# Norms in a two-block transformer kernel: adding squares on VectorE, fewer steps behind the sums, and rows moved behind the heads' step

## The reference, cut to what matters

```python
def rms_norm(x, w):
    y = x * lax.rsqrt(jnp.mean(x * x, axis=-1, keepdims=True) + NORM_EPS)
    return y * w

def modulate(x, g, shift, scale):
    return rmsnorm(x, g) * (1.0 + scale) + shift

def l2norm(t):                       # queries and keys of the delta net, per head
    return t * lax.rsqrt(jnp.sum(t * t, axis=-1, keepdims=True) + EPS)
```

## Time and profile before

| | |
|---|---|
| median of 3 runs | 3462.91 us (3462.8 to 3464.23) |
| profiled execution: its own time | 3464.78 us |
| profiled execution: span | 3463.0 us |
| mean granted clock of PE | 0.967 |
| busy: PE, DVE, ACT, POOL | 3294.6, 2049.1, 1328.1, 528.5 us |

### The profile page before, as it was taken

How to read it: one execution, slowest core, us unless ns; L and a number is a source line. 1 busy time by engine, 2 the same in 40 slices (tenths; PEclk the granted TensorE clock), 3 DMA queues, 4 the chain that set the end, 5 groups by cost and what they waited for, 6 DMA issues and landing times.

```text
span 3463.0 us, 41094 instructions
## 1 busy us (share of the span) xinstructions
PE 3294.6 (95%) x16321; PEld 2722.7 (79%) x16321; DVE 2049.1 (59%) x3543; ACT 1328.1 (38%) x2338; POOL 528.5 (15%) x547
## 2 busy tenths in 40 slices
PE   8999999999999999999899997899898999999998
PEld 5764889998888888888788875778686667778887
DVE  5765987776888888887555435445443345443332
ACT  3131238883444444444322224444443124232221
POOL 0001009971222222221000000000000000000000
PEclk9999999999999999999899998999899999999999
DMA  6426234569999999996355422121121122222222
GB/s 253 138 70 221 74 123 173 191 218 345 335 329 333 338 330 327 338 327 250 105 187 183 144 70 91 58 86 67 64 83 55 41 82 79 90 79 96 96 94 75
DMA packets 190207, 574.42 MB, mean 166 GB/s; under 512 B 16576, under 2 KB 82112, under 8 KB 171712
## 3 DMA queue, kind: packets, MB, share of 16 engines
q1 hardware_dynamic: 152144, 367.96, 30.4%
q0 software_dynamic: 37872, 203.84, 16.0%
HBM read 523.89 MB, written 47.84 MB: 165 GB/s over the span
## 4 chain that ended last, share of the span: by engine, by line
PE 84%; DVE 9%; ACT 3%; POOL 2%; DMA 1%; issue 1%; SPq 0%; DVEq 0%; ACTq 0%; POOLq 0%
PE ps L231 11%; PE ps L232 10%; PE ps L233 10%; PE ps L1602 5%; PE ps L1603 5%; PE ps L1601 5%; PE ps L1362 4%; PE ps L1364 4%; PE ps L1363 4%; PE ps L240 4%; PE ps L581 2%; PE ps L316 2%; PE ps L171 1%; DVE Wl L223 1%; PE ps L584 1%; POOL peerg_OH L1354 1%
## 5 line engine op out<-in xcount | busy, mean ns | idle before, releaser
L223 DVE TENSOR_TENSOR Wl<-W,Wh 128x1024 fp32r<-128x1024 f32 x363 | 438.6, 1209 | 706.5 <-ACT Wh L217 700.3
L217 ACT ACTIVATE Wh<-W 128x1024 fp32r<-128x1024 f32 x363 | 377.6, 1041 | 567.2 <-PE ps L233 532.1
L1362 PE MATMUL ps<-peer_Hh,Wh 128*128 128x384 f32 x1024 | 349.5, 341 | 8.9 <-DVE Wl L223 8.9
L1364 PE MATMUL ps<-peer_Hh,Wl 128*128 128x384 f32 x1024 | 346.3, 338 | 0.0
L1363 PE MATMUL ps<-peer_Hl,Wh 128*128 128x384 f32 x1024 | 346.0, 338 | 0.0
L1570 POOL DMA_INDIRECT peerv_UV<-peer_uv,peer_EX x128 | 209.8, 1639 | 641.1 <-DVE peer_Y L1638 583.5
L1601 PE MATMUL ps<-peerv_VH,peer_HTh 128*128 128x512 f32 x768 | 299.0, 389 | 2.2 <-DVE peer_HTl L1664 2.2
L1603 PE MATMUL ps<-peerv_VH,peer_HTl 128*128 128x512 f32 x768 | 300.5, 391 | 0.0
L1602 PE MATMUL ps<-peerv_VL,peer_HTh 128*128 128x512 f32 x768 | 300.3, 391 | 0.0
L231 PE MATMUL ps<-f_Hh,Wh 128*128 128x512 f32 x672 | 262.3, 390 | 2.2 <-DVE Wl L223 2.2
L233 PE MATMUL ps<-f_Hh,Wl 128*128 128x512 f32 x672 | 261.5, 389 | 0.0
(11 more groups left out here) (497 smaller groups left out, 6499.3 us busy)
## 6 DMA issues: line engine op xcount, KB each, us to landing
W<-peer_u SPq DMA_DIRECT2D x128, 512.0 KB, 8.0
peerv_VR<-peer_v SPq DMA_DIRECT2D x128, 512.0 KB
gates_dram<-peerg_GB SPq DMA_DIRECT2D x12, 2048.0 KB, 7.3
peerv_GR<-gates_dram SPq DMA_DIRECT2D x32, 768.0 KB, 8.6
f_AW<-w_ada POOLq DMA_DIRECT2D x48, 512.0 KB, 4.2
W<-w_gate SPq DMA_DIRECT2D x44, 512.0 KB, 3.2
W<-w_up SPq DMA_DIRECT2D x44, 512.0 KB, 3.2
swa_AW<-w_ada POOLq DMA_DIRECT2D x32, 512.0 KB, 4.5
```

Of the source, the lines that this page charges most:

```text
L217: A.then_inc(e.activation(w_parts(i)[0], w_raw(i), ACT.Copy), ("w_hi", i))
L223: V.then_inc(e.tensor_tensor(lo, w_raw(i), hi.bitcast(F32), SUB), ("w", i))
L1362: e.matmul(o, hi[:, k, :], H2[0][:, k, 0:TD], start=k == 0, stop=False)
L1364: ins = e.matmul(o, lo[:, k, :], H2[0][:, k, 0:TD], start=False, stop=k == 7)
```

## The change

- In six norms DVE adds most squares onto the first one (`add_dve`, a tensor_tensor of 128x512), and PE sums that one tile, called S, beside the rows named in `order`. n2, m2, f2 and ne sum S and row 7 (8 matmuls in place of 32); nf and f1 sum rows 2, 5, 7 and then S (16). n1 keeps all eight rows. All of a norm's matmuls accumulate into four PSUM columns. Row 0 has a slot of its own, the others alternate between two.
- `mean_dve` goes. ACT's root reads the sums in PSUM itself, with 1/D as its scale and epsilon as its bias (a column set once at the start). The diagonal is made in four tensor_scalar of 128x128, and PE broadcasts each quarter as soon as it is there.
- In the loops the blocks of the squares leave their places between the tiles and stand behind the loop.
- In stage delta a row now has two halves on DVE and ACT, and the heads' step stands between them: weight tile, scaling and root first; then the heads; then convolution (DVE), silu, square or drain (ACT). PE's order stays. The root of the rows' norm reads PSUM too, without DVE's addition of epsilon (L2117).

```diff
     class Norm:
...
         def square(self, k):
-            return DG_t[:, 512 * (k % 3):512 * (k % 3) + 512]
+            at = 512 * (k % 2 + 1) if k else 0
+            return DG_t[:, at:at + 512]

         def sq_act(self, e, k):
             self.ready(e, k)
-            if k >= 3:
-                PE.wait_ge(e, (self.tag, "sq", k - 3))
+            if k - 2 in self.adds:
+                V.wait_ge(e, (self.tag, "add", k - 2))
+            elif k > 2:
+                PE.wait_ge(e, (self.tag, "sq", k - 2))
             A.then_inc(e.activation(self.square(k), X[:, k, :], ACT.Square), (self.tag, "sq", k))

+        def add_dve(self, e, k):
+            if k in self.adds:
+                A.wait_ge(e, (self.tag, "sq", k))
+                if k > self.adds[0]:
+                    V.wait_ge(e, (self.tag, "add"))
+                V.then_inc(e.tensor_tensor(self.square(0), self.square(0), self.square(k), ADD), (self.tag, "add", k),
+                           (self.tag, "add"))
+
         def sq_pe(self, e, k):
-            A.wait_ge(e, (self.tag, "sq", k))
+            if k == "S":
+                V.wait_ge(e, (self.tag, "add", self.adds[-1]))
+            else:
+                A.wait_ge(e, (self.tag, "sq", k))
             for tb, sl in enumerate(sl4):
-                ins = e.matmul(self.bank[:, 8 * tb + k:8 * tb + k + 1], self.square(k)[:, sl], ones[:, 0:1],
-                               start=True, stop=True)
+                ins = e.matmul(self.bank[:, tb:tb + 1], self.square(0 if k == "S" else k)[:, sl], ones[:, 0:1],
+                               start=k == self.order[0] and tb == 0, stop=k == self.order[-1], skip_group_check=True)
             PE.then_inc(ins, (self.tag, "sq", k))

-        def mean_dve(self, e):
...
         def root_act(self, e):
-            V.wait_ge(e, (self.tag, "mean"))
-            A.then_inc(e.activation(self.s, self.s, ACT.Sqrt), (self.tag, "root"))
+            V.wait_ge(e, "eps")
+            PE.wait_ge(e, (self.tag, "sq", self.order[-1]))
+            A.then_inc(e.activation(self.s, self.bank[:, 0:4], ACT.Sqrt, bias=eps1, scale=1.0 / D), (self.tag, "root"))

         def root_dve(self, e):
             A.wait_ge(e, (self.tag, "root"))
             V.then_inc(e.reciprocal(self.s, self.s))
             V.wait_ge(e, V.n)
-            V.then_inc(e.tensor_tensor(v4(self.square(8)), bc4(ident), self.s.unsqueeze(2).broadcast_to([128, 4, 128]),
-                                       MUL), (self.tag, "diag"))
+            for tb, sl in enumerate(sl4):
+                V.then_inc(e.tensor_scalar(self.square(8)[:, sl], ident, self.s[:, tb:tb + 1], None, MUL),
+                           (self.tag, "diag", tb))

         def root_pe(self, e):
-            V.wait_ge(e, (self.tag, "diag"))
-            PE.then_inc(e.matmul(self.bank, ones, self.square(8), start=True, stop=True), (self.tag, "rstd"))
+            for tb, sl in enumerate(sl4):
+                V.wait_ge(e, (self.tag, "diag", tb))
+                PE.then_inc(e.matmul(self.bank[:, sl], ones, self.square(8)[:, sl], start=True, stop=True),
+                            (self.tag, "rstd"))
...
     def wout1_pe(e):
...
-            if nb >= 4:
-                n2n.sq_pe(e, nb - 4)
         ada2a.pe(e, 2)
-        for k in range(4, 8):
+        for k in n2n.order:
             n2n.sq_pe(e, k)
     def wout1_dve(e):
...
             for n in range(3 * nb, 3 * nb + 3):
                 ada2a.mac(e, n)
+            n2n.add_dve(e, nb - 1)
             PE.wait_ge(e, ("wout1", nb))
             residual(e, nb, mod1[:, 16:24], ps(4 + nb % 4), ("x1", nb))
...
     def fin_dve(e):
...
             residual(e, k, mod1[:, 40:48], ps(FIN_BANK[k]), ("x2", k))
+            nf.add_dve(e, k - 2)
+        nf.add_dve(e, 6)
         ff1.scales(e)
-        nf.mean_dve(e)
         nf.root_dve(e)
         for k in range(8):
             nf.scale_dve(e, k, X[:, k, :], vec("final_norm_w"), ("x3", k))
+            f1n.add_dve(e, k - 2)
+        f1n.add_dve(e, 6)
...
@@ FeedForward.pe, and wout2_pe alike
-                if nb >= 2:
-                    then.sq_pe(e, nb - 2)
-            then.sq_pe(e, 6)
-            then.sq_pe(e, 7)
+            for k in then.order:
+                then.sq_pe(e, k)
...
@@ FeedForward.dve
                 if n % 3 == 2:
+                    then.add_dve(e, n // 3 - 1)
                     self.x(e, n // 3)
             for nb in range(len(rest) // 3, 8):
+                then.add_dve(e, nb - 1)
                 self.x(e, nb)
@@ wout2_dve
             w_lo(e, (t_wo2 + ff2.all)[n + 2])
+            f2n.add_dve(e, n - 1)
             PE.wait_ge(e, ("wout2", n))
             residual(e, n, mod2[:, 40:48], ps(n % 4), ("x4", n))
...
     def row_steps(rows, make_head):
...
             live = [g for g in live if next(g, "end") != "end"]
+            if rows:
+                next(rows)
     def rows_act(e):
...
-                V.wait_ge(e, ("nr1", m))
-                A.then_inc(e.activation(r, r, ACT.Sqrt), ("nr2", m))
+                if m >= 3:
+                    V.wait_ge(e, ("ndg", m - 3))
+                PE.wait_ge(e, ("nsum", m))
+                A.then_inc(e.activation(r, ps(6 + m % 2)[:, 0:4], ACT.Sqrt, bias=eps1), ("nr2", m))
+            yield
             if n < NROW:
                 kind, h, c = ROWS[n]
     def rows_dve(e):
...
-                PE.wait_ge(e, ("nsum", m))
-                V.then_inc(e.tensor_scalar(r, ps(6 + m % 2)[:, 0:4], 1.0, EPS, MUL, ADD), ("nr1", m))
                 A.wait_ge(e, ("nr2", m))
...
+            yield
             if n < NROW and ROWS[n][0] == "qkv":
                 _, h, c = ROWS[n]
```

More of the change, by code:

```diff
@@ L248, in build @@
     cs1, cs2 = tiny(8), tiny(8)
+    eps1 = tiny(1)
     def mac(e, acc, w, cs, k):
@@ L300, in build, with __init__ @@
     class Norm:
-        def __init__(self, tag, bank, ready):
-            self.tag, self.bank, self.ready, self.s = tag, ps(bank), ready, tiny(4)
+        def __init__(self, tag, bank, ready, order):
+            self.tag, self.bank, self.ready, self.s, self.order = tag, ps(bank), ready, tiny(4), order
+            self.adds = [k for k in range(1, 8) if k not in order]
         def square(self, k):
-            return DG_t[:, 512 * (k % 3):512 * (k % 3) + 512]
+            at = 512 * (k % 2 + 1) if k else 0
+            return DG_t[:, at:at + 512]
@@ L361, in dve @@
         def dve(self, e):
-            self.norm.mean_dve(e)
             self.norm.root_dve(e)
@@ L421, in build @@
     w1 = tiny(8)
-    n1 = Norm("n1", 0, lambda e, k: x_in.wait_ge(e, "x"))
-    n2n = Norm("n2", 0, lambda e, k: V.wait_ge(e, ("x1", k)))
+    n1 = Norm("n1", 0, lambda e, k: x_in.wait_ge(e, "x"), range(8))
+    n2n = Norm("n2", 0, lambda e, k: V.wait_ge(e, ("x1", k)), ("S", 7))
     PA = Phase("ada")
@@ L513, in ada1_dve @@
     def ada1_dve(e):
+        V.then_inc(e.memset(eps1, EPS), "eps")
         con_in.wait_ge(e, "con")
@@ L1713, in fin_pe @@
             PE.then_inc(ins, ("yt", k))
-        for k in range(8):
+        for k in nf.order:
             nf.sq_pe(e, k)
         nf.root_pe(e)
-        for k in range(8):
+        for k in f1n.order:
             f1n.sq_pe(e, k)
@@ L1802, in act, with dve @@
                 then.sq_act(e, k)
-        def dve(self, e, ahead):
+        def dve(self, e, then, ahead):
             tag = self.tag
@@ L2177, in keys_act @@
             yield
+            yield
     def keys_dve(e):
-        yield
-        yield
+        for _ in range(4):
+            yield
         PE.wait_ge(e, ("nbc", 15))
         lat_norm_dve(e, "k", 2, 6)
+        for _ in range(4):
+            yield
+        lat_scale_dve(e, "k", KL, 2, "g_kv_lat_2", 7)
         yield
-        yield
-        lat_scale_dve(e, "k", KL, 2, "g_kv_lat_2", 7)
         yield
@@ L2894, in wout2_pe @@
             pe_three(e, ps(nb % 4), t_wo2[nb], 8, 128, YP, 0, 8, ("wout2", nb))
-            if nb >= 2:
-                f2n.sq_pe(e, nb - 2)
-        f2n.sq_pe(e, 6)
-        f2n.sq_pe(e, 7)
+        for k in f2n.order:
+            f2n.sq_pe(e, k)
     def wout2_act(e):
@@ L2945, in vector @@
         for tag, stage in (("ada1", ada1_dve), ("swa", mix1_dve), ("wout1", wout1_dve),
-                           ("query", query_dve), ("gates", gates_dve), ("dense", dense_dve), ("fin", fin_dve),                            ("ffn1", lambda e: ff1.dve(e, t_ab)), ("mix2", mix2_dve), ("delta", delta_dve), ("state", state_dve),
+                           ("query", query_dve), ("gates", gates_dve), ("dense", dense_dve), ("fin", fin_dve),                            ("ffn1", lambda e: ff1.dve(e, m2n, t_ab)), ("mix2", mix2_dve), ("delta", delta_dve), ("state", state_dve),
                            ("heads", heads_dve),
-                           ("b2", b2_dve), ("wout2", wout2_dve), ("ffn2", lambda e: ff2.dve(e, [])), ("end", end_dve)):
+                           ("b2", b2_dve), ("wout2", wout2_dve), ("ffn2", lambda e: ff2.dve(e, ne, [])), ("end", end_dve)):
             if tag in on:
```

16 lines of the change are left out of this document (5 added, 11 removed).

## The result

| | before | changed |
|---|---|---|
| median of the runs | 3462.86 us (4 runs) | 3410.70 us (4 runs, 3408.83 to 3412.17) |
| profiled execution, span | 3464.78, 3463.0 us | 3408.83, 3406.9 us |
| busy: PE, DVE, ACT | 3294.6, 2049.1, 1328.1 us | 3249.2, 2064.8, 1330.2 us |

The ratio is 0.9855, with a 95% interval from 0.9839 to 0.9871. The prediction was 3415, in a range from 3400 to 3433: 47.8 us of gain were forecast, 52.2 came. The terms of the sum did less well than the sum, as the experiments show.

The account below looks back on a forecast made before the run. PE, busy 95% of the span, was taken to bound the kernel. Norms 32.8 us plus rows 15 gave 47.8 of gain: 3415 us against a median of 3462.9, range 3400 to 3433.

Parts of the forecast that it names:

- Blocks in the stream: m2, f2, ne, n2: square-sum blocks (four matmuls per row) leave the dense stream at 0.9 each, gaining 13.5 plus 2.7 us.
- n2's tail: After n2's last residual fewer blocks remain and one ahead of 'across' goes: 3.4 us gained, plus 1.5 in tile 7.
- The add ahead of the last residual: In m2 and f2 add 6 delays the tail, 2 x 0.65 = 1.3 us lost; ne gains about 0.4.
- f1 and nf: Sums of 16 matmuls instead of 32, with waits between squares, blocks and adds: f1 gains 1.5 us, nf 0.8.
- rival B: Clock falls earlier: eight blocks of n2, ne and nf take 1.8 instead of 0.9, 7 us less gain, 3422; chance 0.10.
- The chain behind the sums: Last block to first scaling takes 2.28 us instead of 3.84: gain 1.55 in each of six norms, 9.3.
- Half the clock in the shorter tails: Sign that the prediction is wrong: PE at half the clock in the new, shorter norm tails.
- n1: Two short DVE operations and one wait leave n1's sums' chain between the adaLN additions: 1.0 us gained (0 to 1.4).
- The rows: Stage delta: PE's waits for L2316 and L2276 lose 12.4 and 5.1 us, less 2.5 for new waits: 15 gained.
- these waits would fall under 10: Sign that the prediction is right: in delta, PE's waits for L2316's counterpart fall under 10 us.
- Rival A: Norms gain, rows don't: the later convolution makes PE wait 1.2 us for squares at twelve rows, 3430; chance 0.21.
- C: Slower: same place, waits of 4 us at each of twelve rows cancel the gain, 5 us gives 3475; chance 0.05.

Follow-up runs that it names:

- e5: Changed kernel, but n2, m2, f2 and ne sum all eight rows on PE between the tiles again; 3446.32 us.
- e3: Changed kernel with no weight split ahead of the last residual of m2 and f2, and f1 summing S ahead of row 7; 3410.67 us.
- e1: Changed kernel with the norms' part alone, the rows of stage delta as before; 3434.88 us.
- e6: Changed kernel with one 128x512 diagonal and one 512-column broadcast, the root still reading the sums; 3415.01 us.
- e4: Changed kernel plus extra 128x128 PE matmuls of two constants, which nothing reads, in the tails of six norms; 3397.20 us.
- e2: Changed kernel with the rows' part alone, the norms as before; 3439.80 us.
- e7: Changed kernel, but on DVE a row stands whole ahead of the heads' step, convolution included; ACT stays split; 3423.67 us.
- e12: Changed kernel with the edits of e3 and e4 together; 3398.73 us.
- e10: Same kernel as e3, run with more rounds; 3406.83 us.

## Why the prediction was right, and where it was not

- **Blocks in the stream.** This was right: 0.9 each was forecast, 0.95 measured (e5). No record of the squares is left between dense tiles, and 192 in all.
- **n2's tail.** This was right in the profiled execution. From the end of tile 7 to the end of the sums it is 3.47 us in place of 6.91, a gain of 3.4 as forecast, and tile 7 itself takes 7.11 in place of 8.81, 1.7 for the 1.5 that was counted:

```profile
320.32 7.11 PE L240 MATMUL ps<-mix_MX,W 128*128 128x512 f32 x16
```

  That the multiply-adds' weights would become late was in no term and no rival; in other executions it takes back 1.7 to 6.5 us.
- **The add ahead of the last residual.** This was right, 0.6 each: from the last dense matmul to the end of the sums it is 4.46 in place of 3.86 in m2, 6.26 in place of 5.65 in f2. What holds the residual is the split, though (e3). ne gained its 0.4.
- **f1 and nf.** f1's sums end 13.78 after nf's first scaling in place of 15.28, a gain of 1.5 as walked. nf gained none of its 0.8. Here rival B held in part: the two last blocks of nf take 3.58 us, at a granted clock of 0.50; before, all eight took 8.56. It held for n2's two blocks as well where the weights came late (3.27 in e1).

```profile
1640.76 3.58 PE L333 MATMUL ps<-consts_sb,DG 128*128 128x1 f32 x16 [0.81 <-ACT DG L317]
```

- **The chain behind the sums.** This step failed: 1.55 for each of six norms, 9.3 in all; measured 0.62 to 0.77 in nf, f1, m2 and f2, 1.36 in n2, 1.06 in ne, 5.3 in all. n2 and ne got more since the clock stayed up longer there: their broadcasts took 1.41 and 1.62. What is wrong is "PE broadcasts each quarter as it comes ... behind the last diagonal remain 0.35 + 0.43". At half the clock a quarter takes 0.52 and the diagonals come every 0.22: PE is the slower of the two, and the quarters queue for 2.08 from the first diagonal on. The prediction's own figures said so: 1.7 for columns, an estimate that no row shows, is 0.43 for a quarter, more than 0.22. e6 gives the quarters 0.3 to 0.4, and e4 shows the 2.4 that the higher level allows in m2. Half the clock in the shorter tails was among the prediction's own signs of being wrong.
- **n1.** There was no gain in place of 1.0. DVE's stream sets the first scaling here: its multiply-adds end at 36.45, the broadcasts at 31.78. Two short operations went from it, but DVE now waits 0.86 for the root, since ACT's table load, 1.28 us, no longer lies ahead of ACT's wait (below).
- **The rows.** The waits were right for the two lines that they were forecast for: 12.0 us less for L2276 (forecast 11.3), 6.3 less for L2316 (6.2; that these waits would fall under 10 did not follow from that term and was wrong). New waits for late squares are 2.0 (2.5). Rival A's place is right, and its price is small, as the walk said; C needed 4 us at every row. A wait of 2.5 for the reciprocal (L2117), which no term had, is gone; the weight split's waits, priced at 0.8 at most, grew by 1.7. The term was too small, 15 for 20 to 23, since the clock was only in its upper bound: fewer waits, and matmuls 6.5 us faster.

So the total was right by luck, through errors that cancel: the chain was 4 too high, n1 1, the rows 5 to 8 too low. e1 and e2 show the same: the norms gave 28.8 of 32.8, the rows 23.9 where 15 were forecast. The clock is in all but one: it fell where the chain was reckoned at full speed, and stayed up where waits went away.

## What to carry to other kernels

Where several pieces of work feed each other in a pipeline, the sum goes by the slower side, at the clock that is granted there: multiply the piece by its count on either engine before one is called hidden. To read a wait, ask what the instruction that ends it waits for itself, and don't stop at its name (e7). When a stream of PE gets shorter, look for transfers that were hidden under it with little to spare; and where short dependent steps leave PE idle, matmuls that compute nothing can be worth their place; too many, ahead of work that is ready, cost time (f1 in e12).

## What the runs showed of the hardware that I had not expected

- In n1 the table load for the root moved behind a wait. Before (first row), it began right behind the last square. The changed kernel has, on ACT (the other two):

```profile
21.72 1.28 ACT L328 ACT_TABLE_LOAD   x1
```

```profile
26.53 1.28 ACT L341 ACT_TABLE_LOAD   x1 [2.83 <-PE ps L333]
27.83 0.27 ACT L341 ACTIVATE small<-ps,small 128x4 f32<-128x4 f32 x1
```

  In the later norms it still begins behind the square (f1 needs none). n1's root is the first one and waits for epsilon as well as for PE; that the second wait is the cause is argued from the code and was not tried apart.
- Where the load is on the path (e4), square to root is 1.31 us: the square ends at 2044.36, the load takes 1.28, the root begins at 2045.67. The Trainium skill (ScalarE: Activation LUTs, section What ACT_TABLE_LOAD costs) gives 1283 ns for the load and about 2.66 us for a whole switch. The load agrees; a switch of 2.66 is not seen in these rows.
- The same kernel's executions differ by 2 to 10 us (e4: 3393.92 to 3401.36; e10: 3400.67 to 3410.01). n2's late weights are one source that the traces show; the stretch from the first gate matmul to the dense stage, 281.6 to 285.4 us long over all kernels, is another, and its cause stays open.
